# Attention's pipeline made one pair of heads shorter: transposes behind the next pair's scores, value products one pair after that

## What is computed

```python
def causal_block_attention(q, k, v, log_forget_cum=None):
    ...
        s = jnp.einsum('bqhd,bkhd->bhqk', q_i, kf) * scale
        if has_decay:
            s = s + args[2][..., :, None] - d_keys[:, :, None, :]
        s = jnp.where(key_pos[None, :] <= q_pos[:, None], s, -jnp.inf)
        p = jax.nn.softmax(s, axis=-1)
        return jnp.einsum('bhqk,bkhd->bqhd', p, vf)
```

## Time and profile before

| | us |
|---|---|
| time, median of 3 runs (2789.77 to 2793.28) | 2790.49 |
| the profiled execution's own time | 2793.99 |
| its span, from first to last instruction | 2792.1 |
| first attention, from the first score matmul to the next stage's DVE work | 105.0 to 133.3 |
| second attention, likewise | 500.5 to 528.8 |

### The profile page before, as it was taken

How to read it: one execution, slowest core, us unless ns; L and a number is a source line. 1 busy time by engine, 2 the same in 40 slices (tenths; PEclk the granted TensorE clock), 3 DMA queues, 4 the chain that set the end, 5 groups by cost and what they waited for, 6 DMA issues and landing times. The chain is left out here.

```text
span 2792.1 us, 31787 instructions
## 1 busy us (share of the span) xinstructions
PE 2194.2 (79%) x13296; PEld 1373.5 (49%) x13297; DVE 660.1 (24%) x1432; ACT 368.9 (13%) x743; POOL 59.4 (2%) x96
## 2 busy tenths in 40 slices
PE   7887769987769968899766666699688997666665
PEld 5563436653338647688422232286477884222222
DVE  4541114621111253453200000022532112000001
ACT  1510011510010031201100000000311011000000
POOL 0200000200000000000000000000000000000000
PEclk9999999999889989999888788899898998878887
DMA  9349997239993410286699999944100446999997
GB/s 389 121 186 428 428 428 322 91 138 429 428 428 153 165 60 1 99 334 246 275 428 428 429 428 428 427 181 155 56 1 1 157 154 286 427 428 428 429 428 314
DMA packets 55834, 779.42 MB, mean 279 GB/s; under 512 B 6840, under 2 KB 7096, under 8 KB 8120
## 3 DMA queue, kind: packets, MB, share of 16 engines
q1 hardware_dynamic: 55736, 778.02, 66.9%
HBM read 776.95 MB, written 1.05 MB: 279 GB/s over the span
## 5 line engine op out<-in xcount | busy, mean ns | idle before, releaser
L1747 PE MATMUL bank<-ring,arena 128*32 128x512 f32 x3136 | 498.3, 772 | 337.8 <-DMA ring<-in_w_exp 334.0
L1747 PEld LDWEIGHTS bank<-ring,arena 128*32 128x32 f32 x3136 | 101.6, 126 | 726.4 <-DMA ring<-in_w_exp 493.8
L1772 PE MATMUL bank<-ring,arena 128*32 128x512 f32 x1568 | 197.0, 641 | 70.1 <-DMA ring<-in_w_exp 47.3
L885 PE MATMUL bank<-xnT,ring 128*128 128x256 f32 x960 | 212.2, 384 | 9.5 <-ACT xnT L368 9.5
L1927 DVE TENSOR_TENSOR arena<-bank,arena 128x256 f32<-128x256 f32 (+1 forms) x33 | 18.3, 554 | 788.1 <-PE bank L1747 561.3
L885 PEld LDWEIGHTS bank<-xnT,ring 128*128 128x128 f32 x960 | 185.3, 193 | 36.9 <-issue 11.2
L1478 PE MATMUL bank<-xnT,ring 128*128 128x256 f32 x768 | 178.9, 387 | 10.3 <-PEq L1013 10.3
L1478 PEld LDWEIGHTS bank<-xnT,ring 128*128 128x128 f32 x768 | 149.5, 195 | 33.2 <-issue 11.9
L1717 PE MATMUL bank<-arena 128*128 128x256 f32 x592 | 145.8, 402 | 3.6 <-DVE arena L1938 3.6
L1717 PEld LDWEIGHTS bank<-arena 128*128 128x128 f32 x592 | 115.6, 201 | 63.1 <-issue 47.7
L1772 PEld LDWEIGHTS bank<-ring,arena 128*32 128x32 f32 x1568 | 50.6, 113 | 186.6 <-issue 96.2
(11 more groups left out here) (339 smaller groups left out, 2235.7 us busy)
## 6 DMA issues: line engine op xcount, KB each, us to landing
ring<-in_w_exp SPq DMA_DIRECT2D x288, 2048.0 KB, 25.7
arena<-in_w_ada SPq DMA_DIRECT2D x24, 2048.0 KB, 11.2
ring<-in_w_in SPq DMA_DIRECT2D x20, 2048.0 KB, 20.9
ring<-in_w_merge SPq DMA_DIRECT2D x18, 2048.0 KB, 8.2
ring<-in_w_o SPq DMA_DIRECT2D x8, 2048.0 KB, 11.6
ring<-in_w_conv SPq DMA_DIRECT2D x6, 2048.0 KB, 26.4
ring<-in_w_rest SPq DMA_DIRECT2D x2, 1696.0 KB, 26.1
small<-in_small SPq DMA_DIRECT2D x2, 1440.0 KB
```

The source lines that it names most:

```text
L885: last = nc.tensor.matmul(o[:, T * j:T * j + T], w[:, k, col:col + P], xnT[:, k, :], start=k == 0, stop=k == KT - 1)
L1747: last = nc.tensor.matmul(o[rows(e), :], Xw[:, k, rows(e)], ring[:, slot(n), at:at + MW], start=k == 0, stop=k == KT - 1)
L1772: last = nc.tensor.matmul(o[rows(e), :], hidT[:, j, rows(e)], ring[:, slot(n), at:at + MW], start=j == 0, stop=j == ft - 1)
```

## The change

PE issues in round i `scores(i)`, `turn(i-1)`, `product(i-2)`. DVE takes a pair's result two heads earlier in its loop, ACT copies a head's transposes one head earlier, and each loop is shorter accordingly. No instruction is added or removed, and buffers and semaphores are as they were.

```diff
-                    for i in range(NPAIR + 3):
+                    for i in range(NPAIR + 2):
                         if i < NPAIR:
                             scores(i)
                         if i == 1:
                             decays()
-                        if 2 <= i <= NPAIR + 1:
-                            turn(i - 2)
-                        if i >= 3:
-                            product(i - 3)
+                        if 1 <= i <= NPAIR:
+                            turn(i - 1)
+                        if i >= 2:
+                            product(i - 2)
...
-                    for n in range(NH + 6):
+                    for n in range(NH + 4):
                         if n < NH:
                             softmax(n)
                         if n == 0:
                             decays()
                         if 1 <= n <= NH:
                             finish(n - 1)
-                        if n % 2 == 1 and n >= 7:
-                            take((n - 7) // 2)
+                        if n % 2 == 1 and n >= 5:
+                            take((n - 5) // 2)
...
-                    for n in range(NH + 3):
+                    for n in range(NH + 2):
                         if n < NH:
                             exps(n)
...
-                        if n >= 3:
-                            to_sbuf(n - 3)
+                        if n >= 2:
+                            to_sbuf(n - 2)
```

## The result

The changed kernel takes 2830.09 us (median of 4 runs, 2826.14 to 2835.41), against 2791.89 us before (4 runs, 2789.77 to 2796.45): a ratio of 1.0136, 95% interval 1.0114 to 1.0158. It is slower, as forecast, but the forecast was 2815.2 with a range up to 2828. The loss is 38 us by the medians and 32.1 us between the two profiled executions (spans 2824.2 and 2792.1), where 24.7 had been worked out. The forecast had started from 2790.49, the median of three runs; with the fourth the kernel before stands at 2791.89, 1.4 us higher.

The account below looks back on a forecast made before the run. PE was taken to bound attention. New waits of 14.84 us less 2.50 us gone gave 12.34 us per attention, 24.7 us for two; added to 2790.5 this made 2815.2 us, range 2809 to 2828.

Parts of the forecast that it names:

- nothing outside attention would take up or add to the loss: Stages outside attention: what one attention gains or loses counts fully, twice, since no transfer is under way during attention.
- The fox rounds' wait: Rounds 4 to 7: PE waits 2.08 us each for a pair's second head before its transposes, 8.32 us per attention.
- The mla rounds: Mla rounds 2 and 3: PE waits 1.60 us each for the pair's second head, 3.20 us per attention.
- Round 1: Behind the decays: PE waits 1.22 us for head 0 and 0.77 us for head 1, together 1.99 us.
- The end: Behind the last pair's scores: PE waits 2.08 us as in fox rounds, then a further 1.33 us for head 15.
- The sum: Per attention: new waits of 14.84 us less 2.50 us of waits gone, net 12.34 us; 24.7 us for two.
- The clock in the new gaps: PE in attention: the forecast went by the trace that the clock stays at 1.00 despite 2.08 us idle per round.
- rival B: Attention: the same waits, and the granted clock falls in some rounds, 2821 to 2834 us; chance 0.25.
- the prediction's own sign of being wrong: Profile of attention: prediction wrong if PE's waits total under 10 us, ACT releases them, or the clock is below 1.00.
- B's upper case: Half of the six rounds with a large wait run at half clock, 18.6 us more, 2834 us.
- Rival C: Attention: transposes find their head ready, so the pipeline is only shorter; 2785.5 us at best, not slower; chance 0.03.

Follow-up runs that it names:

- products first: Changed kernel with PE taking the value products of pair i-2 ahead of the transposes of pair i-1 in each round: 2813.01 us, ratio 1.0059.
- four transposes: Changed kernel with 4 more transposes on PE ahead of the wait for a pair's second head: 2824.52 us, ratio 1.0103.
- three kernels: Changed kernel with 12 transposes, 4 transposes or 4 matmuls more ahead of the wait for a pair's second head: 2823.8, 2824.52 and 2821.97 us.
- early reciprocal: Changed kernel with the reciprocal of a pair's second head ahead of the next pair's first mask on DVE: 2814.49 us, ratio 1.0065.
- POOL's part cut: Changed kernel with POOL multiplying only 2 of 256 columns of a head's second part: 2812.16 us, ratio 1.0058.
- the kernel before with the early reciprocal: Kernel before the change, with a pair's second head's reciprocal ahead of the next pair's first mask on DVE: 2809.61 us, ratio 1.0045.

## Why the prediction was wrong

Its mechanism and its sum held; the clock was weighed wrongly, and the range with it.

- That nothing outside attention would take up or add to the loss: right, 367.19 us between the attentions in both traces.
- The fox rounds' wait: forecast 2.08, measured 2.08 (122.75 - 120.27 - 0.40). The hand-over of 2.48 us behind the scores was found again with other work inside it (2.49, products first), and it moved with POOL's work and with the reciprocal's place.
- The mla rounds: forecast 1.60, measured 1.53. Round 1: forecast 1.22 and 0.77, bracketed 1.05 and 0.63, with 0.1 for the count 1.15 and 0.73.
- The end: forecast 1.33 and no wait before head 14. In the changed kernel it was 0.81 in brackets in both attentions, but PE came later there, at half clock. With the clock held (four transposes) it is 146.02 - 144.30 - 0.40 = 1.32, the transposes within it, and there was no wait before head 14.
- The sum: forecast 12.34 us per attention, measured with the clock held 12.55 (three kernels). As a whole 24.7 against 25.1. What the sum lacks is that a head's three transposes behind a wait cost 0.47 us up to the products (123.22 - 122.75) and not 0.40, seven times in an attention.
- **The clock in the new gaps, rival B**: this step failed. The forecast put the clock's cost at nothing, and the prediction's own sign of being wrong, a clock row below 1.00 in attention, came (0.89 and 0.85). I gave it 0.25 and argued that the work behind the gaps is dense, 3.12 us in a row. The row of 181.40 to 183.40, with 2.0 us of idle time and a fall behind it, was the nearest one in size to the new gap of 2.08, and it pointed the right way. (Its reading was short: 1.3 us of small matmuls lie between that gap and the fall.) The density of the work did not help: behind three of the four fox waits of each attention the clock fell. B's price per round was too high for what happened (3.1 us forecast for a round wholly at half clock, 6.80 - 5.26 = 1.54 measured, since the clock was at 0.50 for 3.3 us only and back for the last scores), but it came in half of the six rounds with a large wait, B's upper case. The sum of it was 4.1 + 5.4 = 9.5 us between traces; 24.7 + 9.5 added to 2790.5 would have been 2824.7. That alone lies inside the range. The median came out at 2830.1, inside rival B's 2821 to 2834, and 2 us over the range, which I had cut at 2828 "with most of B".
- What is left are 5.4 us, from 2824.7 to 2830.1. Of these 1.4 are the fourth run of the kernel before and 0.4 the sum; the other 3.6 stay open. Between the traces the span grew by 32.1 us: 34.6 in the attentions, -1.5 ahead of the first and -1.0 behind the second. The medians differ by 38.2, since the profiled execution was the fastest of the changed kernel's four runs and 2.1 us over the median of the kernel before. The experiments' medians lie from 2.6 us below to 7.2 us above what their attentions account for. Part of this arises where no edit reaches: the first attention began between 102.93 and 107.97 us over the eleven traces. Single runs of the kernel before range from 2787.8 to 2798.7.
- The rule of the Trainium skill (TensorE: Matmul & The Clock Gate, PE-mode transpose), that transposes do not count as busy as matmuls do, would have pointed to rival B, and B came. The runs speak against the reason all the same: 4 or 12 fp32 transposes in the gap held the clock at 1.00, as 4 matmuls did. Going by the rule would have been luck.
- Rival C asked for the second head to be ready 0.40 us behind the scores. The early reciprocal gave waits of 0.25 to 0.70 in brackets and, with the clock held, an attention of 34.56 us, still 6.3 more than before. No run had both the early reciprocal and the cut on POOL, so the other half of C's condition was not tested.

None of the nine kernels beats the one before: it has no idle time on PE in its fox rounds, and all of its waits together are 2.50 us per attention, some 5 us in all.

## What to carry over

How far ahead this software pipeline must run was set by the chain that closes a round. For a pipeline of this kind, write down when the last head's operand is ready after its trigger (here 2.48 us), and take away a stage only if that is less than what PE has to do before it needs it (here 0.40). In an engine that takes its queue in order, count the instructions that stand ahead of the link by accident, as the next head's mask stood ahead of this head's reciprocal. Moving that link helps only where it is waited for: it gained 6.3 us in each attention of the short pipeline and lost 5.2 in the long one.

When a change opens a gap of some 2 us on PE in every round, price the granted clock too, from the row with the nearest gap, and let the range hold it. A few useless transposes in the gap show in one run what the clock's part is.

## What the runs showed of the hardware

- The clock can fall in step with a loop. With waits of 1.94 us in rounds of 5.26, it fell to 0.50 behind three waits in a row, for some 3.3 us of work, and was back at 1.00 by the next wait; a full round became 1.54 us longer in the first attention and 1.62 in the second. With 1.50 us idle in rounds of the same length it stayed at 1.00 in both attentions.
- The length of a gap alone did not tell whether the clock would fall: it held behind single waits of 1.94 us (round 4) and behind waits of 1.52 in rounds of 4.85 us (POOL's part cut), and fell near the end of attention at waits of 1.13 and 0.96 (products first) and of 1.0 and 0.7 (early reciprocal). In the kernel before with the early reciprocal it fell behind a wait of 1.80 and held behind one of 1.79.
- Useless work made the kernel faster: 12 transposes (1.3 us) in each gap took an attention from 44.92 and 46.25 us to 40.85.
- An fp32 matmul of 128 columns cost PE 0.22 us and has two rows in the trace; an fp32 transpose of the same size cost 0.11 us and has one. A stretch's count of rows is not a count of matmuls.
